# Odd layer's values as three fp32r products, with the projection blocks and the heads laid out anew

## The reference

```python
q, k, v, o, z, gates = split(h @ w_in)           # v, o, z: 8 heads x 256
s   = (q k^T) * exp(d - m_row)                   # one direction; the other one is flipped
num = s @ v ; den = sum(s)                       # chunks and state, here written as one sum
h   = num / max(|den|, exp(-m_row))
h   = (h_f + h_b) * sigmoid(o)
y   = (rms_norm(h, per head) * silu(z)) @ w_out
```

## Time and profile before

| | |
|---|---|
| median of three runs | 1777.19 us |
| the profiled execution, its span | 1777.32 us, 1775.5 us |
| TensorE, its weight loads | 97%, 78% busy |
| VectorE, ScalarE, GpSimd | 66%, 52%, 3% busy |
| DMA | 267 MB, 151 GB/s on average |
| the odd layer's blocks and heads | some 630 to 907 us of the span |

### The profile page before, as it was taken

How to read it: one execution, slowest core, us unless ns; L and a number is a source line. 1 busy time by engine, 2 the same in 40 slices (tenths; PEclk the granted TensorE clock), 3 DMA queues, 4 the chain that set the end, 5 groups by cost and what they waited for, 6 DMA issues and landing times. The chain is left out here.

```text
span 1775.5 us, 22881 instructions
## 1 busy us (share of the span) xinstructions
PE 1725.6 (97%) x8547; PEld 1392.6 (78%) x8547; DVE 1170.9 (66%) x2154; ACT 917.4 (52%) x1497; POOL 49.5 (3%) x68
## 2 busy tenths in 40 slices
PE   8999999999998999999999999999999999999998
PEld 3866888777787777777778787788887787878886
DVE  6654566688438467766767775777646867577744
ACT  4332554433326355656656556467534746547743
POOL 0000000000000000000100002000000002000000
PEclk9999999999999999999999999999999999999999
DMA  9466221221325444453544444556555454555562
GB/s 344 152 207 214 96 72 48 72 72 56 134 95 191 138 125 127 149 154 110 164 154 149 143 155 166 171 182 193 190 190 159 137 165 142 184 165 178 190 217 74
DMA packets 115974, 267.24 MB, mean 151 GB/s; under 512 B 5413, under 2 KB 9838, under 8 KB 115673
## 3 DMA queue, kind: packets, MB, share of 16 engines
q1 hardware_dynamic: 111384, 252.26, 43.5%
q0 software_dynamic: 3504, 10.96, 2.1%
q10 hardware_dynamic: 976, 2.57, 0.4%
HBM read 264.63 MB, written 1.14 MB: 150 GB/s over the span
## 5 line engine op out<-in xcount | busy, mean ns | idle before, releaser
L155 DVE TENSOR_TENSOR qw_rest<-weights,qw_lead 128x1024 fp32r<-128x1024 f32 (+2 forms) x428 | 519.9, 1221 | 373.4 <-ACT qw_lead L343 368.1
L343 ACT ACTIVATE qw_lead<-weights 128x1024 fp32r<-128x1024 f32 (+2 forms) x428 | 446.2, 1048 | 454.1 <-PE psum L182 412.9
L182 PE MATMUL psum<-qw_lead,b_h_pair 128*128 128x512 f32 (+1 forms) x960 | 319.7, 398 | 4.0 <-ACT b_gates L3003 1.3
L182 PEld LDWEIGHTS psum<-qw_lead,b_h_pair 128*128 128x128 f32 x960 | 180.3, 188 | 44.7 <-issue 3.7
L182 PE MATMUL psum<-qw_rest,b_h_pair 128*128 128x512 f32 (+1 forms) x480 | 186.2, 388 | 0.0
L175 PE MATMUL psum<-b_h_pair,qw_lead 128*128 128x512 f32 x512 | 178.1, 393 | 2.0 <-DVE b_h_pair L722 2.0
L176 PE MATMUL psum<-b_h_pair,qw_rest 128*128 128x256 f32 x512 | 142.6, 279 | 0.0
L182 PE MATMUL psum<-e_h_lead,qw_lead 128*128 128x512 f32 x320 | 132.0, 413 | 2.2 <-DVE e_qT L1599 1.4
L182 PE MATMUL psum<-e_h_lead,qw_rest 128*128 128x512 f32 x320 | 125.7, 393 | 0.0
L182 PE MATMUL psum<-e_h_rest,qw_lead 128*128 128x512 f32 x320 | 125.0, 391 | 0.0
L175 PEld LDWEIGHTS psum<-b_h_pair,qw_lead 128*128 128x128 f32 x512 | 95.9, 187 | 24.3 <-DVE b_h_pair L722 2.8
(11 more groups left out here) (490 smaller groups left out, 3033.5 us busy)
## 6 DMA issues: line engine op xcount, KB each, us to landing
weights<-in_w_in SPq DMA_DIRECT2D x48, 1024.0 KB, 5.1
weights<-in_o_w_in SPq DMA_DIRECT2D x32, 1024.0 KB, 5.4
weights<-in_w_mlp_up SPq DMA_DIRECT2D x32, 1024.0 KB, 5.5
weights<-in_w_mlp_down SPq DMA_DIRECT2D x32, 1024.0 KB, 4.9
weights<-in_e_w_in SPq DMA_DIRECT2D x26, 1024.0 KB, 5.1
weights<-in_w_mod SPq DMA_DIRECT2D x24, 1024.0 KB, 7.2
weights<-in_e_w_out SPq DMA_DIRECT2D x8, 1024.0 KB, 5.0
weights<-in_o_w_out SPq DMA_DIRECT2D x8, 1024.0 KB, 4.9
```

Of the source, the lines that this page charges most:

```text
L155: return eng.tensor_tensor(self.rest[at], src, self.lead[at].bitcast(F32), ALU.subtract)
L182: mm = nc.tensor.matmul(out, l, r, start=start and i == 0, stop=stop and i == 2)
L343: self.core.nc.scalar.activation(self.buf.lead[self.at(u)], self.raw(u), ACT.Copy).then_inc(self.lead_ready, 1)
```

## The change

Values are stored as lead and rest in one buffer (`Split`), all leads by ScalarE, all rests by VectorE 0.25 places later. The turned probabilities become lead and rest too, with one buffer instead of two (`copies` writes the lead, the new `prob_rests` the rest), and `values` makes three fp32r products of each of its four. Blocks two to four run o gate, z gate, values; their weights are streamed in that order. Heads start at 11.7, 19.7, 28.2, 36.2, 44.2, 52.2, 60.2 and 66.0; `values`, `outs` and `squares` stand 0.2 places later within a job. The rests of finished heads go where the head's o gate was, the leads where the keys were; the wait of the first four turns for `valued` 12 is gone. Two of the turns move to 70.6 and 76.2.

```diff
+def pair_order(i, v, o, z):
+    return (o, z, v) if i else (v, o, z)
...
-        for name, lo in (("o_v", OD_V), ("o_o", OD_O), ("o_z", OD_Z)):
+        for name, lo in pair_order(i, ("o_v", OD_V), ("o_o", OD_O), ("o_z", OD_Z)):
...
-                self.v = (sb(early, "v0", [P, NT, 2 * ML_V]), v1)
+                self.v = Split(nc, early, "o_v", [P, NT, 2 * ML_V])
...
+                with ExitStack() as turned:
+                    hs_rest = turned.enter_context(nc.sbuf_tensor("o_hs_rest", [P, LT, ML_H * ML_V], F32R))
                 self.o_gate = sb(early, "o", [P, LT, ML_H * ML_V])
...
-                self.WT = sb(early, "WT", [P, LT, 2 * SEQ])
+                self.WT = Split(nc, early, "o_WT", [P, 2 * SEQ])
...
         for j, h, t, at in self.jobs(3.9):
             act.wait_ge(self.turned, j + 1)
-            if j >= LT:
-                act.wait_ge(self.valued, j - 1)
-            self.core.nc.scalar.activation(self.odd.WT[:, t, :], self.core.ps[:, self.banks[2], :], ACT.Copy).then_inc(self.WT_ready, 1)
+            if j:
+                act.wait_ge(self.valued, j)
+            self.core.nc.scalar.activation(self.odd.WT.lead[:], self.core.ps[:, self.banks[2], :], ACT.Copy).then_inc(self.WT_ready, 1)
+
+    def prob_rests(self, dve):
+        for j, h, t, at in self.jobs(4.05):
+            yield at
+            dve.wait_ge(self.WT_ready, 2 * j + 1)
+            self.odd.WT.take_rest(self.core.nc.vector, np.s_[:], self.core.ps[:, self.banks[2], :]).then_inc(self.WT_ready, 1)
...
-        for j, h, t, at in self.jobs(4.3):
+        for j, h, t, at in self.jobs(4.5):
...
-                mm = nc.tensor.matmul(ps[:, self.banks[2], 0:ML_V], odd.WT[:, t, b * P:(b + 1) * P], odd.v[h // 2 % 2][:, b, pair_of(h)], start=(b == 0), stop=(b == 3))
+                mm = split_matmul(nc, ps[:, self.banks[2], 0:ML_V], odd.WT.parts(np.s_[:, b * P:(b + 1) * P]), odd.v.parts((slice(None), b, pair_of(h))), b == 0, b == 3)
...
-    starts = [11.7 + 16 * (h // 2) + 6.0 * (h % 2) for h in range(ML_H)]
+    starts = [11.7, 19.7, 28.2, 36.2, 44.2, 52.2, 60.2, 66.0]
...
+    def v_lead(i, g):
+        def out(act, src):
+            if i and g == 0:
+                act.wait_ge(heads.valued, 4 * i)
+            return nc.scalar.activation(odd.v.lead[:, g, :], src, ACT.Copy)
+        return out
...
+                                 dve=lambda g: lambda dve, src: odd.v.take_rest(nc.vector, np.s_[:, g, :], src))
...
+        for part, ticks in pair_order(i, (values, 8.0), (gate_o, 4.0), (gate_z, 4.0)):
+            items.append(Item(**part(at)))
+            at += ticks
...
         pe.wait_ge(norm.scaled, 2 * n + 2)
-        if n < 4:
-            pe.wait_ge(heads.valued, 12)
-    turn = Turn(core, "od_t_", blocks, [57.0, 58.2, 59.4, 60.6, 63.2, 63.9, 70.0, 76.0], (5,),
+    turn = Turn(core, "od_t_", blocks, [57.0, 58.2, 59.4, 60.6, 63.2, 63.9, 70.6, 76.2], (5,),
```

More of the change, by code:

```diff
@@ L2221, with __init__ @@
 class HeadFeatures:
-    def __init__(self, split, first):
-        self.split, self.first = split, first
+    def __init__(self, lead, rest):
+        self.leads, self.rests = lead, rest
     def lead(self, n):
-        return self.split.lead[:, 2 * n:2 * n + 2, :].rearrange("p k t -> p (k t)")
+        return self.leads[:, 2 * n:2 * n + 2, :].rearrange("p k t -> p (k t)")
     def rest(self, n):
-        z = self.first if n < 4 else self.split.rest
-        return z[:, 2 * n:2 * n + 2, :].rearrange("p k t -> p (k t)")
+        return self.rests[:, :, n * ML_V:(n + 1) * ML_V]
     def parts(self, at):
-        lead, rest = self.split.parts(at)
-        return lead, self.first[at] if at[1] < 8 else rest
+        _, k, part = at
+        return self.leads[at], self.rests[:, k % 2, k // 2 * ML_V + part.start:k // 2 * ML_V + part.stop]
 class OddRoom:
@@ L2243, in __init__ @@
         with ExitStack() as c:
-            v1 = sb(c, "v1", [P, NT, 2 * ML_V])
             with ExitStack() as early:
-                self.v = (sb(early, "v0", [P, NT, 2 * ML_V]), v1)
+                self.v = Split(nc, early, "o_v", [P, NT, 2 * ML_V])
                 self.kT = sb(early, "kT", [P, ML_H, 2 * SEQ])
                 self.h = Split(nc, early, "o_h", [P, KC, 2 * SEQ])
+                with ExitStack() as turned:
+                    hs_rest = turned.enter_context(nc.sbuf_tensor("o_hs_rest", [P, LT, ML_H * ML_V], F32R))
                 self.o_gate = sb(early, "o", [P, LT, ML_H * ML_V])
@@ L2252, in __init__ @@
                 self.Dm = sb(early, "decay", [P, LT, 2, 2 * SEQ])
-                self.WT = sb(early, "WT", [P, LT, 2 * SEQ])
+                self.WT = Split(nc, early, "o_WT", [P, 2 * SEQ])
                 self.spread = sb(early, "spread", [P, 2, 2 * SEQ])
-            hs_first = c.enter_context(nc.sbuf_tensor("o_hs_first", [P, 8, SEQ], F32R))
-            self.hsT = Split(nc, c, "o_hsT", [P, 16, SEQ])
+            sb(c, "under_hsT", [P, 2, NT, 2 * ML_V])
+            hs_lead = c.enter_context(nc.sbuf_tensor("o_hs_lead", [P, 16, SEQ], F32R))
         flat = core.hT[:].rearrange("p k t -> p (k t)")
         self.z = flat[:, 0:2048].rearrange("p (i t n) -> p i t n", i=2, t=LT)
-        self.out_src = HeadFeatures(self.hsT, hs_first)
+        self.out_src = HeadFeatures(hs_lead, hs_rest)
         self.gain = flat[:, 2048:3072].rearrange("p (i n) -> p i n", i=2)
@@ L2411, in __init__ @@
         self.tensor = (self.scores, self.turns, self.values)
-        self.vector, self.scalar, self.gpsimd = (self.maxima, self.mixes, self.outs), (self.decays, self.copies, self.squares), (self.spreads,)
+        self.vector, self.scalar, self.gpsimd = (self.maxima, self.mixes, self.prob_rests, self.outs), (self.decays, self.copies, self.squares), (self.spreads,)
     def logs(self):
@@ L2509, in copies @@
             act.wait_ge(self.turned, j + 1)
-            if j >= LT:
-                act.wait_ge(self.valued, j - 1)
-            self.core.nc.scalar.activation(self.odd.WT[:, t, :], self.core.ps[:, self.banks[2], :], ACT.Copy).then_inc(self.WT_ready, 1)
+            if j:
[6 more added lines that the diff above has]
+            self.odd.WT.take_rest(self.core.nc.vector, np.s_[:], self.core.ps[:, self.banks[2], :]).then_inc(self.WT_ready, 1)
     def values(self, pe):
         nc, ps, odd = self.core.nc, self.core.ps, self.odd
-        for j, h, t, at in self.jobs(4.3):
+        for j, h, t, at in self.jobs(4.5):
             yield at
             if t == 0 and h % 2 == 0:
-                self.dense.wait_first(pe, 8 * (h // 2) + 4)
-            pe.wait_ge(self.WT_ready, j + 1)
+                self.dense.wait_first(pe, 8 * (h // 2) + (8 if h else 4))
+            pe.wait_ge(self.WT_ready, 2 * j + 2)
             for b in range(4):
-                mm = nc.tensor.matmul(ps[:, self.banks[2], 0:ML_V], odd.WT[:, t, b * P:(b + 1) * P], odd.v[h // 2 % 2][:, b, pair_of(h)], start=(b == 0), stop=(b == 3))
+                mm = split_matmul(nc, ps[:, self.banks[2], 0:ML_V], odd.WT.parts(np.s_[:, b * P:(b + 1) * P]), odd.v.parts((slice(None), b, pair_of(h))), b == 0, b == 3)
             mm.then_inc(self.valued, 1)
@@ L2526, in outs @@
         odd = self.odd
-        for j, h, t, at in self.jobs(4.7):
+        for j, h, t, at in self.jobs(4.9):
             yield at
             if t == 0 and h % 2 == 0:
-                self.dense.wait_first(dve, 8 * (h // 2) + 6)
+                self.dense.wait_first(dve, 8 * (h // 2) + (2 if h else 6))
             dve.wait_ge(self.valued, j + 1)
@@ L2536, in squares @@
         odd = self.odd
-        for j, h, t, at in self.jobs(5.0):
+        for j, h, t, at in self.jobs(5.2):
             yield at
@@ L2568, in gains @@
             dve.wait_ge(self.gain_in, 16 * (i + 1))
-            self.dense.wait_first(dve, 8 * i + 8)
+            self.dense.wait_first(dve, 8 * i + (4 if i else 8))
             for t in range(LT):
@@ L2628, in odd_layer @@
         at, cs = 16.0 * i, slice(i * BANK, (i + 1) * BANK)
[L2629 to L2636, removed]
+        values = lambda at: dict(**span(range(first[f"o_v{i}"], first[f"o_v{i}"] + 4), at, 2.0), groups=tokens(NT), src=odd.h, act=lambda g, i=i: v_lead(i, g),
+                                 dve=lambda g: lambda dve, src: odd.v.take_rest(nc.vector, np.s_[:, g, :], src))
+        gate_o = lambda at: dict(**span(range(first[f"o_o{i}"], first[f"o_o{i}"] + 4), at, 1.0), groups=tokens(LT), src=odd.h,
+                                 act=lambda g, cs=cs: lambda act, src: nc.scalar.activation(odd.o_gate[:, g, cs], src, ACT.Sigmoid))
+        gate_z = lambda at: dict(**span(range(first[f"o_z{i}"], first[f"o_z{i}"] + 4), at, 1.0), groups=tokens(LT), src=odd.h, act=lambda g, i=i: z_out(i, g))
+        for part, ticks in pair_order(i, (values, 8.0), (gate_o, 4.0), (gate_z, 4.0)):
+            items.append(Item(**part(at)))
+            at += ticks
     dense = Dense(core, "o_in_", items, (0, 1, 2, 3))
```

## The result

The changed kernel takes 1797.53 us, the median of four runs (1795.60 to 1798.62), against 1777.38 for the kernel before in the same comparison (1777.16 to 1777.73, four runs). The ratio is 1.0111, 95% interval 1.0098 to 1.0123: slower by 1.1%, where 1791.0 was predicted, range 1782 to 1800.

A forecast was written before the change was run, and what follows sets the result against it. TensorE, busy 97% of the span, was taken to bound the kernel, with 4.7 us of waits in the stage. New waits of 23.2 us (+18.5) less 4.7 for products gave +13.8 on 1777.2: 1791.0 us, range 1782 to 1800.

The forecast's parts named there:

- Products: Values of the odd layer's stage: twelve fp32r products take 1.43 us a job, not 1.72; 4.7 us saved.
- Added rests and leads: VectorE gets some 16 us more, ScalarE 5 us more in the 230 us stage; by shares both fit.
- the walk: Going through the engines' written queues in order of place with measured step times, to find TensorE's waits in the stage.
- What was put at nothing: Reordered weight loads, their DMAs and GpSimd's row transfers cost nothing; an exposed late weight at most about 2.1 us once.
- Roots among decays: Five heads' roots stand inside the next head's decays: twelve table loads by decays, seven by roots, against eight and four.
- Waits, 23.2 us: New places make TensorE wait 23.2 us in the stage against 4.7; 3.6, 3.3, 4.3 at heads 1, 3, 5.
- The sign "over 3 us": Waits over 3 us before the first turns of heads 1, 3 and 5, released by the mix, would show it right.
- Clock: Rival: one to four long TensorE waits bring half clock, 1.7 to 7 us lost, 1793 to 1798, taken as 1795; chance 0.20.
- Sum: Whole kernel: waits +18.5 less 4.7 for products, +13.8 on 1777.2, makes 1791.0 us; chance 0.60, own range 1786 to 1796.
- Two of the bounds: Twelve products at 1.36 or 2.73 us a job would make the total +12.9 or +33.
- The drain: The skill page's 1380 ns drain per ScalarE table load would add 14 us, about 1805; given no chance of its own.
- Faster: Rival: free quarter of VectorE and ScalarE takes up the new work, three 0.90 us waits end; 1770, chance 0.08.

The follow-up runs named there:

- the run with fp32 products in good places: Changed kernel with all places laid out anew and values multiplied as plain fp32, rests written but not multiplied: 1775.98 us, ratio 0.9982 to the kernel before.
- the clock kept full: Changed kernel with products nobody reads filling TensorE's waits before the first turns of heads 1, 3, 4 and 5: 1791.16 us, ratio 1.0071 to the kernel before.
- the last two experiments: Kernel before, roots of heads 1, 3, 5 moved among decays: 1792.10 us; changed kernel's places with before's plain fp32 work, no rests: 1797.84 us.

## Why the prediction was right in its cause and short in its size

- **Products.** Right: 1.43 us a job, and the run with fp32 products in good places has the 4.6 us back.
- **Added rests and leads, 0.69 us each in the walk.** Right that they matter little for heads 0 to 5, whose turns wait as long with and without them; only the 0.28 us behind the turns of heads 2 and 4 come with them. In the last phase they weigh: 2.39 and 0.69 us in front of the values of heads 6 and 7, and 1.2 in front of a finished head's turn by the list of waits, against 1.67, none and 0.6 without the rests. What was put at nothing, weights and row transfers, was nothing: no wait in TensorE's list is released by one.
- **Roots among decays.** Right: 12 and 7 loads, 2.20 us of VectorE idle in front of head 1's scales, 3.70 us of waiting where 3.6 was forecast. That roots among decays make these waits is shown from three sides (roots later, roots without a load, the kernel before with roots put wrongly), in full at head 1 and for about half at head 3. At head 5 the forecast's account fails for the larger part: 2.22 and 2.41 us stay without the loads and with the roots moved. They go with all places laid out anew, so they belong to the order; which step of it was not tried.
- **Waits, 23.2 us.** Too long by 3.1, counted as the forecast counts them (20.1): head 3 2.71 (forecast 3.3), head 5 3.65 (4.3), head 2 0.96 with the 0.28 behind its turn (1.3), head 4 2.01 likewise (2.2), head 6 1.28 (1.65), head 6's second job 2.81 with the 0.42 in front of its turn (3.15), head 7's first values 0.69 (1.35). Heads 0 and 1 and the finished head's turn are right to 0.1 us; the other places were right and the walk's sizes 0.2 to 0.7 us too long. The sign "over 3 us" failed at head 3. It is not that a slow TensorE hides part of the waits: with the clock kept full the ten long ones come to 19.1 us as well. At head 2 the weight lead behind the decays ends at 735.38, 1.6 us after the unit's first group where the walk has 1.9, and the mix starts 0.4 us sooner; the durations at the other heads were not followed.
- **Clock.** The step that failed. The prediction priced a half-speed stretch rightly (1.7 us for 3.4) and named the waits that would bring it, but set it beside the forecast, as another case with a chance of 0.20, and so put it at nothing in the sum. Its reason against it, that TensorE is dense on both sides, did not hold: TensorE was busy 0.09 of the 2 us from 704.00 and 0.37 of the next two, and the clock fell in these. Of the seven waits over 3 us in the kernel after and in the last two experiments five were followed by half clock, so a term was due, though only as a range. Here it cost 6.7 us by the filled waits (7.6 in the stage), up to 8.5 by the half-clock time.
- **Sum.** 1777.2 - 4.6 + 15.4 gives 1788.0; the clock in the stage (6.7 to 8.5) and 2.4 us outside it make 1797.1 to 1798.9, and the profiled execution, from which the parts are read, took 1798.62. The errors of the two terms have opposite signs, -3.1 and +6.7 to +8.5. The result, 1797.53, lies in the range, 1.5 us above the forecast's own, inside that of the clock rival (1793 to 1798). This is in part luck: with the forecast's waits the same clock and the same 2.4 us would have given 1800 to 1802, at or beyond the range's end. Two of the bounds are added up wrongly: the twelve products at 1.36 and 2.73 us a job make about +12.7 and +34.7, not +12.9 and +33; the forecast does not use them.
- **The drain.** The Trainium skill ("ScalarE: Activation LUTs", What ACT_TABLE_LOAD costs) adds 1380 ns of draining to a switch. The trace after disagrees as the one before did: the root's load at 697.54 starts 0.02 us after the step ahead ends, and the root 0.02 after the load.
- **Faster.** The rival that spare time on VectorE and ScalarE takes up the new work was wrong for these places. It came true with others, at 1770.30, its own figure of 1770.

## What to carry to other kernels

Where engines run in a written order, moving one stream of work against another changes which functions stand side by side on ScalarE: list them, count a table load at each change, and ask which of the loads stand in front of work that TensorE waits for. Follow a long wait back past the releaser that the profile names, and allow in the sum for half clock behind each wait of several microseconds, as a range. When a change that saves work is slower, run its places without its work: if they are as slow, keep the work and lay out the places.

## What the runs showed of the hardware

Waits of much the same length did and did not bring the clock down. In the kernel after, 2.71 us of waiting at head 3 was followed by 3.4 us at half clock, and so were 1.28 and 1.40 us close together at head 6; 2.39 us in front of head 6's second values was not. With the clock kept full at the other heads, the same 1.28 and 1.40 us at head 6 were not. In all stages of the matrix-memory layer profiled here, five of the seven waits over 3 us were followed by half clock, and five of the nine from 2.2 to 2.8 us. The closest pair is head 5: 3.65 us of waiting up to 832.66 in the kernel after, 3.66 us up to 832.72 in the change's places with before's work, with TensorE idle throughout the 2 us from 830.00 in both. The stretch behind, first after, then with before's work:

```profile
834.00:836.00 2.00, 2.00 (x6) 1.52 (x6) 1.82 (x2) 0.09 (x1) 0.00 (x0) 0.50 0.45 184
```

```profile
834.00:836.00 2.00, 2.00 (x9) 1.30 (x8) 0.94 (x1) 0.01 (x1) 0.00 (x0) 1.00 0.46 188
```

In the query stage, whose code did not change, a wait of 2.67 us from 558.95 was followed by 6.8 us at half clock:

```profile
560.00:562.00 2.00, 0.27 (x2) 0.30 (x3) 1.94 (x4) 2.00 (x6) 0.00 (x0) 1.00 1.06 393
562.00:564.00 2.00, 1.65 (x12) 1.24 (x10) 1.09 (x5) 2.00 (x5) 0.00 (x0) 0.85 1.03 311
564.00:566.00 2.00, 1.37 (x6) 1.40 (x7) 1.48 (x5) 1.43 (x3) 0.00 (x0) 0.50 0.72 278
```

In the kernel before the same wait, 2.64 us from 560.48, was not:

```profile
560.00:562.00 2.00, 0.75 (x7) 0.55 (x5) 2.00 (x2) 2.00 (x5) 0.00 (x0) 1.00 1.04 386
562.00:564.00 2.00, 0.77 (x6) 0.77 (x6) 1.93 (x7) 2.00 (x4) 0.00 (x0) 1.00 1.09 367
564.00:566.00 2.00, 1.09 (x8) 0.77 (x6) 1.10 (x6) 1.52 (x5) 0.00 (x0) 1.00 1.00 342
```

So waits of equal length can cost a stage a few microseconds more or less, and a stage that was not touched can differ between two kernels. What decides it was not tried.
